# A three-phase encoder layer on one core: input rows also fetched in a turned layout, and the routing product cut into four products of 32 columns

## The reference

```
h    = rmsnorm(x) * g_mix                    # (1536, 1024)
proj = h @ w_in                              # (1024, 2496): rq, rk, rv, rg (512 each), cq 256, ckv 128, kr 64
ret_out = silu(rg) * groupnorm(retention(rope(rq), rope(rk), rv))     # 8 heads, both directions, chunks of 128
mla_out = attention(latent queries from cq, latent keys and values from ckv, rotary key kr)   # 4 heads
x = x + concat(ret_out, mla_out) @ w_out
t = rmsnorm(x) * g_ffn
group  = argmax(softmax(t @ w_router_group))             # 4 groups
expert = top 2 of (t @ w_router_expert) in that group    # 8 in each group
x = x + sum over the 2 experts of gate * (silu(t @ w_g) * (t @ w_u)) @ w_d
y = rmsnorm(x) * g_final
```

## Time and profile before

| | |
|---|---|
| median of 3 runs | 1566.23 us (1562.38 to 1566.72) |
| the profiled execution: its time | 1563.33 us |
| its span | 1561.8 us |
| TensorE matmuls busy | 1438.2 us, 92% of the span |
| TensorE weight loads busy | 1193.5 us, 76% |
| VectorE busy | 1091.8 us, 70% |
| ScalarE busy | 871.1 us, 56% |
| GpSimd busy | 283.3 us, 18% |
| DMA, mean over the span | 207 GB/s; near 380 GB/s from about 940 us on |
| mean granted TensorE clock | 0.969 |

### The profile page before, as it was taken

How to read it: one execution, slowest core, us unless ns; L and a number is a source line. 1 busy time by engine, 2 the same in 40 slices (tenths; PEclk the granted TensorE clock), 3 DMA queues, 4 the chain that set the end, 5 groups by cost and what they waited for, 6 DMA issues and landing times.

```text
span 1561.8 us, 22918 instructions
## 1 busy us (share of the span) xinstructions
PE 1438.2 (92%) x8088; PEld 1193.5 (76%) x8088; DVE 1091.8 (70%) x1645; ACT 871.1 (56%) x1148; POOL 283.3 (18%) x270
## 2 busy tenths in 40 slices
PE   6999999999988899986999959999999999999993
PEld 4888788888876678775888847787787877878771
DVE  5666766343456676673466669888888888888886
ACT  6434444334445554453434437777777777777764
POOL 0000111111133000000122131511121221222431
PEclk9999999999999999998999969999999999999996
DMA  7232322222121110013466338999999999999997
GB/s 242 88 100 95 129 89 70 89 81 75 48 88 48 53 30 14 28 48 113 137 216 241 108 149 309 381 373 381 379 383 384 382 375 379 383 380 375 384 345 296
DMA packets 77483, 322.84 MB, mean 207 GB/s; under 512 B 13542, under 2 KB 22118, under 8 KB 52834
## 3 DMA queue, kind: packets, MB, share of 16 engines
q1 hardware_dynamic: 60722, 273.77, 46.8%
q0 software_dynamic: 16688, 48.10, 10.1%
HBM read 278.77 MB, written 51.80 MB: 212 GB/s over the span
## 4 chain that ended last, share of the span: by engine, by line
DMA 22%; PE 12%; DVE 11%; issue 6%; ACT 2%; DVEq 0%; ACTq 0%; SPq 0%; POOLq 0%; POOL 0%
DMA plain<-in_w_down 20%; DVE split L1812 8%; PE acc L96 3%; PE acc L97 3%; PE acc L98 3%; PE acc L2008 1%; ACT split L2519 1%; PE acc L1999 1%; DMA s_x_mid<-plain 1%; ACT shared L1806 1%; DVE plain L2630 0%; DMA plain<-s_h_rows,plain 0%; DVE x_late L2630 0%; DVE shared L1812 0%; DMA plain<-s_x_mid 0%
## 5 line engine op out<-in xcount | busy, mean ns | idle before, releaser
L1806 ACT CAST shared<-plain 128x2048 fp32r<-128x2048 f32 x190 | 361.9, 1915 | 111.5 <-DMA plain<-in_w_up 76.9
L96 PE MATMUL acc<-shared,split 128*128 128x512 f32 x952 | 381.5, 401 | 15.1 <-DVE split L2065 10.3
L98 PE MATMUL acc<-shared,split 128*128 128x512 f32 x952 | 373.0, 392 | 0.0
L1812 DVE TENSOR_TENSOR split<-plain,shared 128x2048 fp32r<-128x2048 f32 x126 | 282.6, 2283 | 0.6 <-ACT shared L1806 0.6
L96 PEld LDWEIGHTS acc<-shared,split 128*128 128x128 f32 x952 | 180.3, 189 | 52.6 <-DVE split L2065 10.5
L98 PEld LDWEIGHTS acc<-shared,split 128*128 128x128 f32 x952 | 179.7, 189 | 38.7
L96 PE MATMUL pa<-shared,a_xT_hi 128*128 128x512 f32 (+1 forms) x480 | 194.0, 404 | 4.2 <-DVE a_w_lo L747 3.3
L97 PE MATMUL acc<-split 128*128 128x512 f32 x504 | 196.5, 390 | 0.0
L98 PE MATMUL pa<-shared,a_xT_lo 128*128 128x512 f32 (+1 forms) x480 | 187.1, 390 | 0.0
L97 PE MATMUL acc<-shared,split 128*128 128x512 f32 x448 | 176.2, 393 | 0.0
L1812 DVE TENSOR_TENSOR shared<-plain,shared 128x2048 fp32r<-128x2048 f32 x64 | 145.9, 2281 | 3.2 <-ACT shared L1806 3.2
(11 more groups left out here) (322 smaller groups left out, 2521.0 us busy)
## 6 DMA issues: line engine op xcount, KB each, us to landing
plain<-in_w_gate SPq DMA_DIRECT2D x64, 1024.0 KB, 9.8
plain<-in_w_up SPq DMA_DIRECT2D x64, 1024.0 KB, 11.6
plain<-in_w_down SPq DMA_DIRECT2D x64, 1024.0 KB, 10.8
a_x_sb<-in_x SPq DMA_DIRECT2D x24, 512.0 KB, 4.1
s_mid<-a_kv SPq DMA_DIRECT2D x12, 512.0 KB, 2.9
a_kv<-s_mid SPq DMA_DIRECT2D x12, 512.0 KB, 3.6
plain<-s_mixT SPq DMA_DIRECT2D x12, 512.0 KB, 7.0
plain<-in_x SPq DMA_DIRECT2D x12, 512.0 KB, 3.9
```

Of the source, the lines that this page charges most:

```text
L96: pe.matmul(out, st_hi, mv_hi, start=first, stop=False)
L98: return pe.matmul(out, st_lo, mv_hi, start=False, stop=last)
L1806: eng.copy(self.w_hi[j // 2][:, cols], self.source(j)).then_inc(self.s_whi[j], 1)
L1812: eng.tensor_tensor(self.w_lo[j // 2][:, cols], self.source(j), self.w_hi[j // 2][:, cols].bitcast(F32), ALU.subtract).then_inc(self.s_wlo ...
```

## The change

The host lays x out a second time, turned: `x_turned`, where tile n holds on partition p the 8 slices of 128 tokens that `transpose_x` used to make. Both passes fetch the turned tile into one buffer `x_turned`; the row layout goes to one buffer `x_row` and is fetched in the first pass only. `transpose_x` is gone. `hi_of_x` and `lo_of_x` read the turned tile from SBUF, one instruction of 1,024 columns each. In the mixing stage each of the 8 routing products becomes four, of 32 stationary columns each, which write to 32 partitions of the output each.

```diff
-        s_x = [sem("x0"), sem("x1")]
-        s_xt, s_hi, s_lo = sem("xt"), sem("hi"), sem("lo")
+        s_row, s_x, s_hi, s_lo = sem("row"), sem("x"), sem("hi"), sem("lo")
...
+            def load_row(t):
+                if t:
+                    sp.wait_ge(s_sq, t)
+                sp.dma_start(x_row, x_all[t]).then_inc(s_row, 16)
+
             def load_x(n):
-                if n >= 2:
-                    sp.wait_ge(s_xt, 2 * (n - 1))
-                    sp.wait_ge(s_sq, min(n - 1, N))
-                sp.dma_start(x_sb[:, n % 2, :], x_all[n % N]).then_inc(s_x[n % 2], 16)
+                if n:
+                    sp.wait_ge(s_lo, n)
+                sp.dma_start(x_turned, x_turned_all[n % N]).then_inc(s_x, 16)
...
             for m in range(NST):
                 load_w(m)
+            load_row(0)
             load_x(1)
             for m in range(NST, 2 * KD):
                 load_w(m)
-            load_x(2)
+            load_row(1)
...
             sp.dma_start(gn_row[:], gn_g.partition_broadcast(P)).then_inc(s_tabs, 16)
-            for n in range(N):
-                if n:
-                    load_x(n + 2)
-                if n:
-                    keep_kv(n - 1)
+            load_x(2)
+            for n in range(1, N):
+                if n + 1 < N:
+                    load_row(n + 1)
+                load_x(n + 2)
+                keep_kv(n - 1)
...
-            def transpose_x(n):
-                pe.wait_ge(s_x[n % 2], 16 * (n // 2 + 1))
-                if n:
-                    pe.wait_ge(s_lo, 2 * n)
-                for b in range(2):
-                    for j in range(4):
-                        k = 4 * b + j
-                        ins = pe.transpose(pX[b][:, j * P:(j + 1) * P], x_sb[:, n % 2, k:D:KD], ident[:])
-                    ins.then_inc(s_xt, 1)
-
...
-                project(V, t, pV[t % 2], low)
-                transpose_x(t + 1)
-                project(V, t, pV[t % 2], high).then_inc(s_pv, 1)
+                project(V, t, pV[t % 2], range(KD)).then_inc(s_pv, 1)
...
             def hi_of_x(n):
-                for b in range(2):
-                    act.wait_ge(s_xt, 2 * n + b + 1)
-                    nc.scalar.copy(xT_hi[:, n % 2, b * 512:(b + 1) * 512], pX[b][:]).then_inc(s_hi, 1)
+                act.wait_ge(s_x, 16 * (n + 1))
+                if 2 <= n <= N + 1:
+                    act.wait_ge(s_pk, n - 1)
+                elif n > N + 1:
+                    act.wait_ge(s_pg, n - 1 - N)
+                nc.scalar.copy(xT_hi[:, n % 2, :], x_turned).then_inc(s_hi, 1)
...
             def lo_of_x(n):
-                for b in range(2):
-                    cols = slice(b * 512, (b + 1) * 512)
-                    dve.wait_ge(s_hi, 2 * n + b + 1)
-                    nc.vector.tensor_tensor(xT_lo[:, n % 2, cols], pX[b][:], xT_hi[:, n % 2, cols].bitcast(F32),
-                                            ALU.subtract).then_inc(s_lo, 1)
+                dve.wait_ge(s_hi, n + 1)
+                nc.vector.tensor_tensor(xT_lo[:, n % 2, :], x_turned, xT_hi[:, n % 2, :].bitcast(F32),
+                                        ALU.subtract).then_inc(s_lo, 1)
...
                 for k in range(KD):
-                    ins = pe.matmul(pr[:, 0:NG + NE], hT[:, k * P:(k + 1) * P], w_r[:, k, :],
-                                    start=k == 0, stop=k == KD - 1)
+                    for q in range(4):
+                        some = slice(q * P // 4, (q + 1) * P // 4)
+                        ins = pe.matmul(pr[some, 0:NG + NE], hT[:, k * P + some.start:k * P + some.stop], w_r[:, k, :],
+                                        start=k == 0, stop=k == KD - 1, tile_position=(0, some.start))
```

More of the change, by code:

```diff
@@ L140, in bank, with phase_project @@
         return self.acc[:, 512 * i:512 * (i + count)]
-def phase_project(nc, block, sems, space, lat, x_all, w_in, g_mix, g_q, g_kv, rope, ident_d, log_decay, gn_g, dist_d, index_d, span_d,
+def phase_project(nc, block, sems, space, lat, x_all, x_turned_all, w_in, g_mix, g_q, g_kv, rope, ident_d, log_decay, gn_g, dist_d, index_d, span_d,
                   mid, mixT, w_cat):
@@ L157, in phase_project @@
         w_lo = [half.rearrange("p (k n) -> p k n", k=KD) for half in w_lo]
-        x_sb = words("a_x_sb", Space.WORK, 2 * D).rearrange("p (a n) -> p a n", a=2)
+        x_row, x_turned = words("a_x_row", Space.WORK, D), words("a_x_turned", Space.WORK + D, D)
         xT_hi = rounded("a_xT_hi", Space.WORK + 2 * D, 2 * D).rearrange("p (a n) -> p a n", a=2)
@@ L328, in _ @@
                     sp.wait_ge(s_pq, N)
-                    sp.wait_ge(s_xt, 4 * N)
                     lat.load_weights(sp)
@@ L499, in _ @@
             pe.wait_ge(s_const, 32)
-            transpose_x(0)
             for t in range(N):
-                pe.wait_ge(s_lo, 2 * (t + 1))
+                pe.wait_ge(s_lo, t + 1)
                 if t >= 2:
                     pe.wait_ge(s_vev, t - 1)
-                project(V, t, pV[t % 2], low)
-                transpose_x(t + 1)
-                project(V, t, pV[t % 2], high).then_inc(s_pv, 1)
+                project(V, t, pV[t % 2], range(KD)).then_inc(s_pv, 1)
                 if t:
@@ L515, in _ @@
                 n = N + t
-                pe.wait_ge(s_lo, 2 * (n + 1))
+                pe.wait_ge(s_lo, n + 1)
                 if t:
@@ L536, in _ @@
                     outputs(t - 1)
-                if t + 1 < N:
-                    transpose_x(n + 1)
-                else:
+                if t + 1 == N:
                     turn_queries(t, 1)
@@ L574, in square @@
             def square(t):
-                act.wait_ge(s_x[t % 2], 16 * (t // 2 + 1))
+                act.wait_ge(s_row, 16 * (t + 1))
                 one = slice(t, t + 1)
@@ L578, in square @@
                     act.wait_ge(s_root, t)
-                nc.scalar.activation(junk, x_sb[:, t % 2, :], ACT.Square, accum_out=ssq[:, one]).then_inc(s_sq, 1)
+                nc.scalar.activation(junk, x_row, ACT.Square, accum_out=ssq[:, one]).then_inc(s_sq, 1)
                 act.wait_ge(s_sq, t + 1)
@@ L2722, in build @@
             block = first.enter_context(nc.Block())
-            rest = phase_project(nc, block, sems, space, lat, d["x"], d["w_in"], d["g_mix"], d["g_q"], d["g_kv"], d["rope"],
+            rest = phase_project(nc, block, sems, space, lat, d["x"], d["x_turned"], d["w_in"], d["g_mix"], d["g_q"], d["g_kv"], d["rope"],
                                  d["ident"], d["log_decay"], d["gn_g"], d["dist"], d["index"], d["spans"], mid, mixT,
@@ L2747 @@
     x = np.concatenate([np.asarray(inputs["x_prompt"])[0], np.asarray(inputs["x_sample"])[0]], 0)
-    arrays = {"x": x.reshape(TILES, P, D), "g_final": inputs["g_final"], **tables()}
+    turned = x.reshape(TILES, P, P, KD).transpose(0, 2, 3, 1).reshape(TILES, P, D)
+    arrays = {"x": x.reshape(TILES, P, D), "x_turned": turned, "g_final": inputs["g_final"], **tables()}
     arrays.update({name: np.asarray(inputs[key])[0] for name, key in WEIGHTS.items()})
```

1 line of the change is left out of this document (removed).

## The result

The changed kernel takes 1541.36 us (median of 4 runs, 1536.02 to 1545.12), and the kernel before took 1565.15 beside it (4 runs). The profiled execution of after took 1545.12 us (span 1543.6), the slowest of its four; that of before took 1563.33. So the spans of the two traces are 18.2 us apart, not 23.8.

A forecast was written before the change was run, and what follows sets the result against it. TensorE was taken to bound the passes and mixing stage. Transposes -18.0, launch +5.0 and routing product +5.3 gave -7.7 us, 1558.5 on the 1566.2 median; own range 1554 to 1562, 8-in-10 range 1546 to 1564.

The forecast's parts named there:

- What bounds the kernel: Both passes and mixing stage: TensorE is nearly always busy, so its saved or added work changes the time, barring new waits.
- Gains given back: Rival, chance 0.13: a new wait replaces the transposes in one pass, losing 8 to 9 us; kernel about 1566 to 1567.
- slower: Rival, chance 0.07: each narrow routing pair still costs 0.106 us, +63 us over 12 tiles, 1616 us.
- the price of the routing product: Mixing stage: 64 pairs at 0.030 us, from the 64-column state product; +0.44 us a tile, +5.3 us for 12.
- The lower bound: Routing product, mixing stage: 0.015 us a pair if four overlap, -0.51 us a tile, -6.1 us for 12.
- four at once: Rival, chance 0.23: the 32-column routing products overlap four deep at 0.015 us a pair; sum -19.1 us, 1547 us.
- The transposes: Removed blocks: 10 at 0.80 us in the first pass, -8.0; 10 at 0.90 in the second, -9.0.
- The term of tile 13: Handover to the second pass: an earlier weight piece shortens TensorE's 2.0 us wait; bounds 0 and 2.0, taken as 1.0.
- The split of x: Both passes: ScalarE's and VectorE's 1,024-column reads from SBUF, 1.03 and 1.22 us, cost nothing, covered by TensorE's products.
- The launch: Kernel start: exponentials wait for tile 2's x and square, state product 5.4 us later; net +5.0 us, bounds 3.5 to 7.5.
- a few tenths forward: Very start: ScalarE no longer waits for first transposes, so weight pieces and tables come earlier; 0.4 us gained.
- The clock at the launch: Lower clock lasts some 5.8 us into the denser work; a later start pays about the same, so nothing added.

The follow-up runs named there:

- the two parts alone: Kernel before with only the turned x and no transposes, 1552.33 us; kernel before with only the routing product cut in four, 1554.27 us.
- changed again: The changed kernel itself, unaltered, run and profiled a second time beside the launch experiments: 1541.32 us.
- tables first: Changed kernel with ScalarE's table exponentials moved ahead of the upper part and square of tile 2: 1537.02 us.
- Rows later: As tables first, with row layouts of tiles 0 and 1 fetched after the 16 weight pieces and the tables, their squares and inverses moved too: 1534.34 us.
- Turns back: Changed kernel with eight unused identity transposes put back into each values product of the first pass's 12 tiles: 1551.38 us.

## Why the prediction was wrong

**What bounds the kernel** held. TensorE stayed without idle time in the passes, and the two parts alone gave 11.5 and 9.6 us as cuts of its work. "Gains given back" and "slower" fell: no engine became late for it in any steady stretch.

**The step that failed** is the price of the routing product: "I take the 64-column row, since it has the same alternation of output parts", 0.030 us a pair, +0.44 us a tile and +5.3 in all. It measured 0.009 us a pair, -0.90 us a tile and -10.8. Those 16.1 us are by themselves the whole gap between the forecast of -7.7 and the measured -23.8; the other terms' errors, below, happen to cancel (-1.2, -1.35 and +2.8 us). The alternation was not the same: the 64-column row goes to and fro between two halves, the new product goes round four groups of half the width. Half the columns brings 0.029 to 0.015 with two groups in turn, and four groups in turn instead of two bring 0.015 to 0.009. The earlier trace rows held the hint, as the rival said: half the columns at 3.5 times the pace is more than the columns explain, so the overlap was in the row already. The prediction's "30 ns at its fastest" is the row's average: the single starts of the same 32 pairs are 0.006 and 0.053 us apart by turns. The lower bound was no bound either, by a slip in its working: its words have two halvings, for half the columns and for four groups at once instead of two, but 0.015 is 0.030 halved once. Halved twice it is 0.0075, which gives 63 x 0.0075 + 0.25 - 1.70 = -0.98 us a tile and -11.7 in all, near the -10.8 that came. The low end of the forecast's own range, 1554, does not follow either: with launch, tile 13 and pair all at their low bounds the sum is 1552, and its 0.025 us a pair is in no row. The entry and exit of 0.25 us did hold (1.02 - 63 x 0.009 = 0.45 from the L98 on, of which 0.23 is the ordinary step). The right mechanism was the rival "four at once", with 1547 us, and that too was 6 us too high, by the same slip.

**The transposes** were right in kind and a little small: 0.92 us in the first pass instead of 0.80, 10 blocks, -9.2 instead of -8.0; in the second 0.90 as forecast, -9.0. The term of tile 13 was taken as 1.0 of a possible 2.0 and measured 2.35: 0.77 by the earlier weight piece, and 1.58 because the clock no longer falls behind the wait. The bound had counted only the wait. That the clock stays up because the transposes are gone is not shown (last section).

**The split of x** cost nothing, as forecast.

**The launch** was a loss as forecast, by the step described, and that step was sized right: 5.2 us in the one profile, and 4.3 us of time between changed again and tables first, against 5.4 and 5.0. But the state product came 6.6 to 10.2 us late (7.8 in changed again), since the table itself landed later by 1.3 to 4.9 us (2.4). The prediction had the weight pieces "a few tenths forward". It looked at ScalarE's wait for the transposes, which is gone, and left out that the new row layout of tile 0, 0.5 MB, goes out ahead of x of tile 1 and ten weight pieces, and that x of tile 1 waits for the single buffer until 8.38 us (5.26 before). ScalarE now waits 3.05 us at 13.8 where before it waited 0.64 at 13.1, and the last of the ten pieces is issued by 21.02 us (20.76 in changed again) instead of 19.64. The rest of the delay is in the table's own way: it takes 7.6 and 7.0 us from issue to landing, 5.1 before. What each transfer costs of this was not separated.

Rows later gives 2.7 us, but not all of that is the row layout's. Its last weight piece is issued by 17.10 us, 3.7 earlier than in changed again. Its seventh piece lands at 13.07 us, as before the change and 0.7 to 1.3 us earlier than in after and changed again (14.32); x of tile 1 goes out as late there (8.31 us), so this part is the row layout's. Some 2.6 us more are the first square and its table load, which no longer stand between the weight pieces, and these the kernel before has as well (14.49 to 17.13 us). So by the trace the greater part of what rows later gains is a gain of its own and not a repair of the change; no run measures the two apart.

The clock at the launch, which the prediction put at nothing, did come to nothing. In the kernel before the granted clock is 0.50 until nearly 44.6 us, 5.8 behind the first state product; after, it is 0.50 to 54 us and 0.88 from 54 to 56, again between 5 and 6 behind that product. The second state product follows 15.13 us behind the first instead of 16.12, less by about one block.

With the measured terms the sum is -9.2 - 2.35 - 9.0 - 10.8 + 7.8 = -23.6 us, with the launch of changed again. That it meets the 23.8 so closely is in part luck: beside changed again the kernel before is 22.6 us longer, and the two profiles are 21.3 apart. The sum leaves out 1.2 us that TensorE waits less at the last tile of the first pass (0.38 us instead of 0.94 and 0.67) and the 3.7 us lost between the passes and the mixing stage, and the experts' stage scatters by 2 us. So some 3 us of it is uncertain.

## What to carry to other kernels

When the trace's nearest row is used as a price, ask what made that row fast before it is scaled: here two groups in turn, where the new code has four. A product whose moving operand is short (36 columns here) is set by its weight loads; cutting it by columns paid when neighbours in the stream went to different groups of output partitions (0.90 us a tile), and brought nothing when one group was finished before the next. A fetch that is moved ahead in a queue "hidden" by later work must be followed to everything behind it in that queue, and to the in-order engine that waits for the last of it.

## What the hardware showed that was not expected

A plain 32-bit product of 32 stationary and 36 moving columns, a weight load and a matmul, can be issued every 0.009 us when the four groups of output partitions take turns, though each instruction's own record is ten and twenty times as long. Weight loads (PEld) and matmuls (PE) of the routing product's line after (ns min/median/max):

```profile
L1999 PEld LDWEIGHTS acc<-plain x768: 106/109/113, 747.7 to 890.6; 128*32 128x32 f32 x192
L1999 PE MATMUL acc<-plain x768: 198/200/220, 747.7 to 890.6; 128*32 128x36 f32 x192
```

So the busy time of such a row says nothing of its cost; only the distance from start to start does. And a wait of about 2 us at the handover is followed by products at the lower clock (granted clock 0.50 from 205 to 208 us in the kernel before) in the two profiles whose second pass still holds the transposes, and by none in the nine of the turned layout. Turns back, which has such transposes in the first pass alone, shows none either (3.25 us to the next transposes). Two things differ ahead of the wait: the two profiles have the transposes of tile 13 there (198.07 us in before), and they wait longer at the last tile of the first pass (0.94 and 0.67 us in before, 0.38 in after). No run parts them, so what keeps the clock up stays open.
